# Encoder step on one core: lo parts of the gated ups spread over VectorE's gate round and GpSimd, and one wait per out unit

## The reference, cut to what matters

```python
x = x + rmsnorm(jnp.concatenate([h_m, attn], axis=-1) @ w_out, g_post_mix)
h = rmsnorm(x, g_pre_ffn)
gate, up = jnp.split(h @ w_ffn_in, 2, axis=-1)
return x + rmsnorm((jax.nn.silu(gate) * up) @ w_ffn_out, g_post_ffn)
```

## Time and profile before

| | |
|---|---|
| median of 3 runs | 3055.79 us (3046.68 to 3056.41) |
| profiled execution, its own time | 3057.72 us |
| its span | 3055.9 us |
| mean granted TensorE clock | 0.973 of 2.4 GHz |
| busy: TensorE / VectorE / ScalarE / GpSimd | 96% / 54% / 32% / 47% |
| feed-forward rounds, layers 0 and 1 | about 840 to 1492 us and 2348 to 3005 us |

### The profile page before, as it was taken

One profiled execution on the slowest core, in us unless ns is written; L12 is line 12 of the kernel. 1 busy time (PEld: TensorE's weight loads), 2 busy tenths in 40 slices (PEclk: granted clock), 3 DMA queues, 4 the chain that ended last, 5 costly groups with the idle time before them and its releaser, 6 DMA issues.

```text
span 3055.9 us, 45786 instructions
## 1 busy us (share of the span) xinstructions
PE 2922.1 (96%) x17057; PEld 2699.5 (88%) x17057; DVE 1656.0 (54%) x2215; ACT 989.1 (32%) x1926; POOL 1433.8 (47%) x1132
## 2 busy tenths in 40 slices
PE   8999999999999999999899999999999999999998
PEld 7999867788999999899789998676989998999997
DVE  7433345546755556555683334365476565555557
ACT  4222224523133333333341223245132333333333
POOL 2222233232477777767422223322425776766772
PEclk9999979999999999999999999899999999999999
DMA  5121210021111111111322112100321111111113
GB/s 166 38 42 33 37 30 1 1 95 67 64 42 52 45 41 52 44 41 41 106 85 52 30 30 36 30 1 8 106 88 39 42 50 46 41 41 41 52 44 128
DMA packets 211566, 154.92 MB, mean 51 GB/s; under 512 B 40856, under 2 KB 195112, under 8 KB 210672
## 3 DMA queue, kind: packets, MB, share of 16 engines
q1 hardware_dynamic: 194304, 111.29, 13.8%
q10 hardware_dynamic: 17136, 41.89, 3.6%
HBM read 128.56 MB, written 24.59 MB: 50 GB/s over the span
## 4 chain that ended last, share of the span: by engine, by line
PE 31%; issue 28%; POOLq 21%; POOL 12%; DVE 5%; ACT 1%; DVEq 1%; DMA 0%; ACTq 0%
PE acc L772 7%; PE acc L776 7%; PE acc L775 7%; POOL slab_lo L692 5%; POOLq L709 3%; POOLq L704 3%; POOLq L699 3%; POOL slab_raw L710 2%; POOLq L713 2%; POOLq L719 2%; POOLq L716 2%; POOLq L722 2%; POOL small_lo L692 2%; POOLq L655 1%; POOLq L658 1%
## 5 line engine op out<-in xcount | busy, mean ns | idle before, releaser
L692 POOL TENSOR_TENSOR slab_lo<-slab_raw,slab_hi 128x512 fp32r<-128x512 f32 (+1 forms) x376 | 415.5, 1111 | 191.1 <-ACT slab_hi L1942 155.8
L557 POOL TENSOR_TENSOR slab_hi<-slab_raw,ones 128x1024 fp32r<-128x1024 f32 x63 | 123.3, 1958 | 680.2 <-PE acc L772 513.5
L772 PE MATMUL acc<-act_hi,slab_hi 128*128 128x352 f32 x1296 | 426.6, 329 | 7.9 <-ACT residual L1666 5.2
L776 PE MATMUL acc<-act_lo,slab_hi 128*128 128x352 f32 x1296 | 416.4, 321 | 0.0
L775 PE MATMUL acc<-act_hi,slab_lo 128*128 128x352 f32 x1296 | 415.7, 321 | 0.0
L1326 PE MATMUL acc<-act_hi,slab_hi 128*128 128x352 f32 x992 | 339.1, 342 | 58.2 <-DVE work L2631 57.3
L1329 PE MATMUL acc<-act_hi,slab_lo 128*128 128x352 f32 x992 | 332.1, 335 | 0.0
L1330 PE MATMUL acc<-act_lo,slab_hi 128*128 128x352 f32 x992 | 331.2, 334 | 0.0
L1942 ACT ACTIVATE slab_hi<-slab_raw 128x512 fp32r<-128x512 f32 (+1 forms) x372 | 191.3, 543 | 408.3 <-DMA slab_raw<-in_w_ffn_in 161.4
L692 POOL TENSOR_TENSOR small_lo<-slab_raw,small_hi 128x256 fp32r<-128x256 f32 (+1 forms) x224 | 223.0, 996 | 190.5 <-ACT small_hi L1942 154.7
L2728 DVE TENSOR_TENSOR branch<-acc,branch 128x704 f32<-128x704 f32 x288 | 256.9, 892 | 88.1 <-PE acc L1394 74.0
(11 more groups left out here) (511 smaller groups left out, 7358.0 us busy)
## 6 DMA issues: line engine op xcount, KB each, us to landing
slab_raw<-in_w_ffn_in SPq DMA_DIRECT2D x152, 256.0 KB, 2.9
slab_raw<-in_w_in SPq DMA_DIRECT2D x40, 512.0 KB, 3.9
slab_raw<-in_w_ffn_out SPq DMA_DIRECT2D x80, 256.0 KB, 2.5
x_spill<-residual ACTq DMA_DIRECT2D x2, 4224.0 KB, 12.4
residual<-x_spill ACTq DMA_DIRECT2D x2, 4224.0 KB, 14.2
f_spill<-residual ACTq DMA_DIRECT2D x2, 4224.0 KB, 11.5
slab_raw<-in_w_out SPq DMA_DIRECT2D x16, 512.0 KB, 4.6
slab_raw<-in_w_ffn_in SPq DMA_DIRECT2D x12, 512.0 KB, 3.7
```

What stands on the lines that cost most here:

```text
L557: pool.tensor_tensor(hi, raw, ONES[:, 0:1].broadcast_to([P, SLAB]), ALU.mult)
L692: pool.tensor_tensor(lo, QUAD[q][:, c0:c1], hi, ALU.subtract).then_inc(unit_ready, 1)
L772: mm = pe.matmul(out, wh, HH[:, x], start=k == 0, stop=False)
L776: mm = pe.matmul(out, wh, HL[:, x], start=False, stop=k == KT - 1)
```

## The change

VectorE's nine lo parts at the end of `up_round` go. Four of the six `small_lo` parts now stand at the head of the next `gate_round`, before L2631; the other two stand in `between()`, behind L2631 and before L2634, with the drain that counts `g_ready`. The three `g_t_lo` parts go to GpSimd, which makes them behind the gate round's `weave` and before the first `weave` of the outs, after a wait for the ninth hi part, with a drain that counts `g_ready` too; all waits on `g_ready` count two per body. In `half_round` TensorE waits for A11, S3 and S2 one by one instead of S2 for all.

```diff
 # GpSimd, in the loop over bodies
                     weave(made, 1 + 3 * b, GATE_SLOTS)
+                    pool.wait_ge(g_hi, G_HI + l * HIS_ALL + 4 + 9 * b + 9)
+                    for i in range(3):
+                        pool.tensor_tensor(GTL[i][:, :], GTF[i][:, :], GTH[i][:, :], ALU.subtract)
+                    pool.drain().then_inc(g_ready, 1)
                     weave(made + 8, 2 + 3 * b, OUT_SLOTS[0], 0, 256, False)
...
 # TensorE, half_round
-                    made_by(S2)
+                    made_by(A11)
                     pe.wait_ge(a_out, A_OUT + 2 * (l * ROUNDS + r))
                     short(0, [(slots[A11], g_part_of(0, 0))], True, True, unit_used).then_inc(a_done, 1)
+                    made_by(S3)
                     pe.wait_ge(y_out, Y_OUT + 2 * (l * ROUNDS + r))
                     short(4, [(slots[S3], (GTH[1][:, :], GTL[1][:, :]))], True, True).then_inc(y_done, 1)
+                    made_by(S2)
                     pe.wait_ge(x_out, X_OUT + 3 * (l * ROUNDS + r))
...
-                    pe.wait_ge(g_ready, G_READY + l * (4 + BODIES) + 4 + b + 1)
+                    pe.wait_ge(g_ready, G_READY + l * (4 + 2 * BODIES) + 4 + 2 * b + 2)
...
 # VectorE, gate_round
-                    chains(r, c12, c21, c22, lambda: None, lambda: None)
+                    his = l * HIS_ALL + 4 + 9 * b
+                    lo = lambda count, j, n: g_lo_part(count, unit_of(RL, j, n), unit_of(RLF, j, n), unit_of(RH, j, n))
+
+                    def between():
+                        lo(his + 5, 0, 1)
+                        lo(his + 8, 1, 0)
+                        dve.drain().then_inc(g_ready, 1)
...
+                    lo(his + 1, 0, 0)
+                    lo(his + 2, 0, 2)
+                    lo(his + 3, 1, 1)
+                    lo(his + 4, 1, 2)
+                    chains(r, c12, c21, c22, between, behind)
...
 # VectorE, end of up_round
                     dve.tensor_tensor(GTF[2][:, :], f(1, 0), GTF[0][:, :], ALU.subtract).then_inc(g_part, 1)
-                    lo(his + 1, 0, 0)
-                    lo(his + 2, 0, 2)
-                    lo(his + 3, 1, 1)
-                    lo(his + 4, 1, 2)
-                    lo(his + 5, 0, 1)
-                    g_lo_part(his + 7, GTL[1][:, :], GTF[1][:, :], GTH[1][:, :])
-                    lo(his + 8, 1, 0)
-                    dve.drain()
-                    g_lo_part(his + 9, GTL[0][:, :], GTF[0][:, :], GTH[0][:, :])
-                    g_lo_part(his + 9, GTL[2][:, :], GTF[2][:, :], GTH[2][:, :])
-                    dve.drain().then_inc(g_ready, 1)
```

More of the change, by code:

```diff
@@ L1352, in long_round @@
                         wait_set(l, 1, SET_USES[1])
-                        pe.wait_ge(g_ready, G_READY + l * (4 + BODIES) + 1)
+                        pe.wait_ge(g_ready, G_READY + l * (4 + 2 * BODIES) + 1)
                     else:
@@ L1358, in long_round @@
                     if prologue:
-                        pe.wait_ge(g_ready, G_READY + l * (4 + BODIES) + 2)
+                        pe.wait_ge(g_ready, G_READY + l * (4 + 2 * BODIES) + 2)
                     else:
@@ L1367, in long_round @@
                     if prologue:
-                        pe.wait_ge(g_ready, G_READY + l * (4 + BODIES) + 3)
+                        pe.wait_ge(g_ready, G_READY + l * (4 + 2 * BODIES) + 3)
                     pe.wait_ge(x_out, X_OUT + 3 * (l * ROUNDS + r) + 1)
@@ L1375, in long_round @@
                     if prologue:
-                        pe.wait_ge(g_ready, G_READY + l * (4 + BODIES) + 4)
+                        pe.wait_ge(g_ready, G_READY + l * (4 + 2 * BODIES) + 4)
                     pe.wait_ge(y_out, Y_OUT + 2 * (l * ROUNDS + r) + 1)
@@ L2641, in chains, with g_lo_part @@
                     dve.drain()
+                def g_lo_part(count, lo, src, hi):
+                    dve.wait_ge(g_hi, G_HI + count)
+                    return dve.tensor_tensor(lo, src, hi, ALU.subtract)
                 def gate_round(b):
@@ L2646, in gate_round, with behind @@
                     c12, c21, c22 = unit_of(W2, 0, 1), unit_of(W2, 1, 0), unit_of(W2, 1, 1)
-                    chains(r, c12, c21, c22, lambda: None, lambda: None)
+                    his = l * HIS_ALL + 4 + 9 * b
[4 more added lines that the diff above has]
+                        dve.drain().then_inc(g_ready, 1)
+                    def behind():
+                        pass
+                    lo(his + 1, 0, 0)
[3 more added lines that the diff above has]
+                    chains(r, c12, c21, c22, between, behind)
                     dve.wait_ge(y_done, Y_DONE + 2 * r + 2)
                     dve.tensor_tensor(c21, bank(4, TG), c21, ALU.add).then_inc(y_out, 1)
-                def g_lo_part(count, lo, src, hi):
-                    dve.wait_ge(g_hi, G_HI + count)
-                    return dve.tensor_tensor(lo, src, hi, ALU.subtract)
                 def up_round(i, last=False):
```

## The result

| | before | changed |
|---|---|---|
| executions timed beside each other | 3046.7, 3055.8, 3056.4, 3056.7 | 2921.2, 2924.0, 2937.2, 2939.7 |
| median | 3056.1 us | 2930.6 us |
| profiled execution | 3057.7 us | 2939.7 us |
| ratio, 95% interval | | 0.9596 (0.9555 to 0.9637) |

The kernel is 4.0% faster. In a second set on another occasion the changed kernel's median was 2943.7 us of six (experiment e1), ratio 0.9649.

A forecast was written before the change was run, and what follows sets the result against it. TensorE's matmuls at the granted clock plus its gaps were taken to bound the kernel. Savings of 3.4 (S1), 0.9 (half round) and 1.9 us (clock), 6.2 a body, times 18 gave 112 us: 2945 us forecast, range 2934 to 2957.

The forecast's parts named there:

- The stall at S1: Gate round: TensorE's wait for VectorE's L2631 goes whole, 3.30 us a body and about 0.1 us of resuming.
- the half rounds' gap: Second half round: TensorE's wait for a GpSimd lo part goes, 0.83 us a body and 0.1 us of resuming.
- The clock: Feed-forward bodies: TensorE's falls to 1.2 GHz behind the gaps vanish, giving back all 1.89 us a body.
- What is late next: Gate round: the two parts in `between()` delay nothing; L2634 ends with 1.1 us of slack before S4, cost 0.
- GpSimd's trio: The three g_t_lo parts on GpSimd take 3.3 us with the drain; the outs' units keep 2.0 us slack, cost 0.
- A rule against it: Skill's advice to keep elementwise work on VectorE would call the trio's move a loss of about 1 us a body, 18 us.
- The pair behind the trio: Rival: `between()`'s two VectorE parts wait for GpSimd's whole trio, S4 starts 1.4 us late, 25 us, 2970 us; chance 0.05.
- GpSimd sets the pace: Slower rival: the trio on GpSimd stalls the half rounds and lengthens each body 3.5 us, 3120 us; chance 0.05.

The follow-up runs named there:

- e1: The changed kernel run again with no edit: median 2943.7 us of six, ratio 0.9649 to the kernel before.
- e3: The changed kernel with the single wait for S2 put back at the head of each half round: 2957.4 us, ratio 0.9708.
- e5: The changed kernel with all six small_lo parts on VectorE ahead of L2637 (L2631 before the change) and `between()` empty: 2943.6 us, ratio 0.9665.
- e7: The changed kernel with four more 352-column subtractions on VectorE ahead of L2637, each with a drain: 3015.6 us, ratio 0.9903.
- e10: The changed kernel with e8's added matmuls, plus three more GpSimd operations of 352 columns ahead of the trio in each body: 2932.3 us.
- e11: The changed kernel with e8's added matmuls, plus six more GpSimd operations of 352 columns ahead of the trio in each body: 2974.9 us.
- e4: The changed kernel with the three g_t_lo subtractions on VectorE, behind the y sum, instead of on GpSimd: 2934.5 us, ratio 0.9638.
- e8: The changed kernel with two 128-column identity matmuls behind each of seven heads of the sample's q projection: 2926.0 us, ratio 0.9605.
- e9: The kernel before the change with only e8's added matmuls: 3039.1 us, ratio 0.9977.
- e2: The kernel before with only the half rounds' one-by-one waits for A11, S3 and S2: 3021.4 us, ratio 0.9927.

## Why the prediction was right, and where it was wrong

- *The stall at S1* (3.4 us a body) and *the half rounds' gap* (0.9): both rows went whole. e3 measures the second alone at 0.93.
- *The clock* (1.9 us): whole. The granted clock is 1.00 in all periods; e5 to e7 show that it followed the idleness. The 1.9 is an average over falls of two lengths: a period of before takes 67.7 us without a fall, about 69.3 with one of 3.4 us and 70.5 with one of 6.8.
- *What is late next* and *GpSimd's trio*: L2637, the pair and the units came within 0.1 to 1 us of the reckoned times, and e10 and e11 found the slack of 2.0 us at 2.3.
- *A rule against it.* The trio cost 3.04 us on GpSimd for 352 columns each, 0.94 us where undisturbed, above the estimate of 0.77 from the Trainium skill, "GPSIMD Engine Reference", 3.1 Elementwise. By the measure of TensorE the move was neither loss nor gain: e4 has the same body without it. The same rule's advice, elementwise work to VectorE, would have cost nothing here.
- *The pair behind the trio*: fell. The pair took 2.39 us and ended 1.7 us before the trio did. Its first part met the 512-column subtraction ahead of the trio; the second ended 0.38 us behind the trio's first subtraction, and the trio's second took 1.24 us instead of 0.94. So VectorE gets in between two of GpSimd's operations.
- *GpSimd sets the pace*: fell, by e10 and e11.

The sum, 18 x 6.2 = 112 us, stands: 113 us by e8 and e9.

**The step that failed** is the forecast's own range, "2934 (the fastest run before was 9 us under the median) to 2957". It took three executions of the kernel before as the measure of how far executions lie apart, "about 0.3%, 9 us", and it subtracted the 112 us from the profiled one, as if all outside the rounds would stay as it was there. That execution had the clock at 1.2 GHz for 37 us in layer 0's attention stage and for 20 us in layer 1's (the 7 and the 8 in the row of the clock); the prediction passed over both as dips "in a few slices only", without a term. (By its own rule the low end would have been 2945 - 9 = 2936.)

The runs showed 25 us between executions of the changed kernel (2921.2 to 2946.2, median 2938.4 of ten) and 34 us for the one before. With e8's matmuls in the attention stages 4 and 7 us are left (e8, e9), so most of it comes from falls in stages that the change does not touch. The first up round's start, with the same code ahead of it, varies between 824.5 and 840.6 us over nine profiles, and between 827.6 and 829.7 us in the four with e8's edit.

A low end near 2920 would have followed from asking what the profiled execution would take without the falls of the clock in the attention stages: 2946 less 16 us for layer 0 (840.2 to 824.5) and, by estimate, 7 to 11 for layer 1 (from the last body of layer 0 to the first of layer 1 the profile before takes 954.4 us, e9 947.6 and e2 942.0). That the first four executions fell outside the range was partly luck of the draw: two of the four were among the fastest (2921.2 and 2924.0), and the median of all ten, 2938.4, lies inside it.

Left open: why some executions escape the fall in the narrow matmuls. What the clock responds to there was not tried beyond e8 and e9. Between the 48 matmuls of 32 columns stand 16 small ones by identity (L1056 and L1058 of the changed kernel, 15 of them transposes), one behind every three; whether the narrow ones or the transposes let the clock fall, no run tells.

## What to carry to other kernels

Where a busy engine waits once per loop turn for an in-order queue, look at what stands ahead of the late instruction and ask of each whether it is wanted sooner; here reordering one queue was worth more than a second engine's help. Price a wait of TensorE with the clock behind it, since shortening it from 3 to under 2 us already brings most of the fall back. Before giving a range, account for the clock in the stages that a change leaves alone: they can move the total by more than the terms still in doubt.

## What the runs showed of the hardware that I had not expected

The clock fell with TensorE hardly idle. In e1 it was busy for all of the 3.80 us ahead of the fall at 388.8 us, with matmuls of 32 columns and a transpose behind every three; two matmuls of 128 columns behind each head kept it at 2.4 GHz. They are not free: with them the first up round starts at 827.6 to 829.7 us, where it starts at 824.5 to 825.4 in the three profiles without a fall, and at 829.5 to 840.6 in the six with one. So they cost some 4 us in layer 0, and a fall 5 to 16. This timeline of e1 shows the fall: the same instruction takes 0.26 us, then 0.38.

```profile
388.46 0.26 PE L745 MATMUL acc<-cq_hi,slab_lo 128*128 128x32 f32 x1
...
388.89 0.38 PE L745 MATMUL acc<-cq_hi,slab_lo 128*128 128x32 f32 x1
```

The Trainium skill, "TensorE: Matmul & The Clock Gate", What's actually happening, says that the clock follows how busy the engine has recently been. The trace agrees for the long waits (a fall at each of e7's 18 waits of 2.8 us and more, none at e5's of 0.2); for the narrow matmuls, "busy" as the profile counts it doesn't foretell the fall.

e8's edit makes the changed kernel steadier. Whether it is also faster is not shown: it has 2926.0 us against 2938.4 over the changed kernel's ten executions, but the two never ran in one set, and its ratio to the kernel before, 0.9605, lies between the changed kernel's two, 0.9596 and 0.9649.
